# An expert's tail prepares the next expert's split operands, and each expert's code gets a short opening

## The reference, cut to what matters

```
logits = t @ w_router + b_router                 # t: 256 x 1024
top_val, top_idx = top_k(logits, 2); gates = softmax(top_val)
for each expert e, for the tokens x routed to it:
    y = (silu(x @ w_gate_e[e]) * (x @ w_up_e[e])) @ w_down_e[e]     # D_FF = 3584
out[token] += gate * y
```

## Time and profile before

| | before |
|---|---|
| median of three runs | 1839.72 us (1830.52 to 1842.34) |
| the profiled execution | 1832.89 us, of it a span of 1831.1 us |
| mean granted TensorE clock | 0.917 |
| busy: PE, DVE, ACT, POOL | 87%, 39%, 30%, 3% of the span |
| HBM read | 482.66 MB, mean 266 GB/s over the span |
| the chain that ended last | PE 78%, DMA 9%, issue 4%, DVE 4%, ACT 2% |
| idle PE ahead of the eight experts | 5.76, 10.71, 7.29, 0, 7.24, 5.16, 12.38, 5.90 us |

### The profile page before, as it was taken

One profiled execution on the slowest core, in us unless ns is written; L12 is line 12 of the kernel. 1 busy time (PEld: TensorE's weight loads), 2 busy tenths in 40 slices (PEclk: granted clock), 3 DMA queues, 4 the chain that ended last, 5 costly groups with the idle time before them and its releaser, 6 DMA issues.

```text
span 1831.1 us, 30902 instructions
## 1 busy us (share of the span) xinstructions
PE 1598.6 (87%) x12644; PEld 1288.1 (70%) x12645; DVE 710.6 (39%) x1017; ACT 545.7 (30%) x749; POOL 63.2 (3%) x66
## 2 busy tenths in 40 slices
PE   5999997999999999967566799989998749999894
PEld 4777776999987687746344687548897538888552
DVE  2162115555532431140000787116665015666212
ACT  2122114343321321020000676115654015545201
POOL 0010000000000100010000000000000000000002
PEclk8998598999999986898787899999999879999998
DMA  9632255744534133268999999999667997555794
GB/s 364 258 111 97 92 190 206 306 187 170 198 103 188 58 128 137 93 253 362 424 424 425 425 411 389 407 424 377 267 249 278 387 422 327 230 207 230 284 424 167
DMA packets 74563, 488.94 MB, mean 267 GB/s; under 512 B 9792, under 2 KB 13920, under 8 KB 16544
## 3 DMA queue, kind: packets, MB, share of 16 engines
q1 hardware_dynamic: 72176, 479.94, 65.2%
q10 hardware_dynamic: 1648, 4.59, 0.7%
q0 software_dynamic: 576, 2.10, 0.4%
HBM read 482.66 MB, written 3.93 MB: 266 GB/s over the span
## 4 chain that ended last, share of the span: by engine, by line
PE 78%; DMA 9%; issue 4%; DVE 4%; ACT 2%; POOL 1%; SPq 1%; ACTq 0%; POOLq 0%; DVEq 0%
PE PG L1278 9%; DMA arena<-in_experts 5%; PE Y L905 5%; PE PG L1388 4%; PE PG L1322 4%; PE TRB L1322 4%; PE Y L1290 4%; PE Y L1350 4%; PE Y L913 3%; PE Y L1162 3%; PE PG L869 3%; PE PG L870 3%; PE PG L871 3%; DMA ring<-in_experts 3%; PE TRB L1328 3%
## 5 line engine op out<-in xcount | busy, mean ns | idle before, releaser
L1278 PE MATMUL PG<-ring,mixT 128*32 128x128 f32 (+1 forms) x1920 | 115.2, 345 | 63.3 <-issue 63.3
L1471 ACT ACTIVATE parts<-ring 128x2048 fp32r<-128x2048 f32 x84 | 158.5, 1906 | 12.4 <-PE Y L871 8.2
L1278 PEld LDWEIGHTS PG<-ring,mixT 128*32 128x32 f32 (+1 forms) x1920 | 88.6, 136 | 93.6 <-issue 77.9
L2257 DVE COPY arena<-TRB 128x64 f32<-128x64 f32 (+1 forms) x70 | 17.6, 251 | 338.7 <-PE TRB L1264 338.7
L1471 ACT ACTIVATE rope<-PG 64x128 f32<-64x128 f32 (+2 forms) x84 | 27.1, 324 | 376.1 <-PE PG L1278 351.7
L1278 PE MATMUL PG<-arena,mixT 128*32 128x128 f32 (+1 forms) x1664 | 100.3, 349 | 41.7 <-issue 41.7
L869 PE MATMUL PG<-h_parts,parts 128*128 128x256 f32 x448 | 127.5, 285 | 10.2 <-DVE parts L2133 10.2
L870 PE MATMUL PG<-h_parts,parts 128*128 128x256 f32 x448 | 127.3, 284 | 0.0
L871 PE MATMUL PG<-h_parts,parts 128*128 128x256 f32 x448 | 127.1, 284 | 0.0
L1278 PEld LDWEIGHTS PG<-arena,mixT 128*32 128x32 f32 (+1 forms) x1664 | 78.1, 138 | 68.6 <-issue 55.5
L2133 DVE TENSOR_TENSOR parts<-ring,parts 128x2048 fp32r<-128x2048 f32 x42 | 95.9, 2292 | 25.6 <-ACT parts L1471 25.6
(11 more groups left out here) (375 smaller groups left out, 2909.4 us busy)
## 6 DMA issues: line engine op xcount, KB each, us to landing
ring<-in_experts SPq DMA_DIRECT2D x168, 1024.0 KB, 13.0
arena<-in_experts SPq DMA_DIRECT2D x168, 1024.0 KB, 16.4
ring<-in_weights SPq DMA_DIRECT2D x116, 1024.0 KB, 5.8
ring<-in_weights SPq DMA_DIRECT2D x4, 512.0 KB, 4.1
ypairs<-hT ACTq DMA_DIRECT2D x3, 512.0 KB, 5.3
tok<-in_x SPq DMA_DIRECT2D x1, 1024.0 KB, 8.8
result<-scr SPq DMA_DIRECT2D x2, 512.0 KB, 2.6
ring<-in_weights SPq DMA_DIRECT2D x2, 432.0 KB, 6.7
```

The source lines that it names most:

```text
L1278: last = mm(bank[i * n:(i + 1) * n, 0:width], xe[:, k, 0:n], w[k // 4][:, k % 4, i * width:(i + 1) * width], start=(k == 0), stop=(k == KD ...
L1471: return nc.scalar.activation(out_, in_, func, **kw)
```

## The change

Every expert's code becomes two bodies. The six openings lie one behind the other right after the comparisons; behind them lie the six rests. An opening ends in a branch to its own rest, for which a hint is given at the opening's start, and the rest branches to `next` as before.

- PE's opening: whole, the first half (4 of 8 channel blocks) of the first gate-and-up; wide and split, the first unit's high product.
- ACT's opening: whole, the first silu; wide and split, the fourth high part. The first three high parts of an expert are made in the rest of the expert before, ahead of the copy out of `Y`, whatever the next form is (for the first expert, ahead of the loop; behind the eighth, three more, on what the slots hold, which nothing reads). Wide rests begin with a small Silu (`silu_table`).
- DVE's opening: whole, the first product and turned copy, after a wait for the three high parts; wide and split, four low parts. The next expert's tokens (192 columns, `tokens_split`) are parted in the rest of the expert before, ahead of the copy out of `Y`; for 256 the other columns in the opening.
- POOL gathers 64 columns to a buffer of their own (`xe`, for the whole forms), then all 256 to `mixT`; a ninth gather to `mixT` follows.
- PE's whole form waits for the second and third high part in its first two stages, since ACT reads the slots that these stages release.

```diff
         ccol = sb("ccol", [P, KD, 32])
-        s4 = sb("s4", [P, T])
+        strip = sb("strip", [P, 2 * T])
+        s4 = strip[:, 0:T]
...
-        diag = sb("diag", [P, TB, P])
+        diag = strip[:, T:2 * T].rearrange("p (b t) -> p b t", b=TB)
...
-        xe = mixT
+        xe = strip[:, :].rearrange("p (k t) -> p k t", k=KD)
...
-            for n in sorted(NVAR, key=lambda n: n != first_variant):
+            layout = sorted(NVAR, key=lambda n: n != first_variant)
+            for n in layout:
                 with nc.body(label(n), valid_engines=own):
+                    on = eng.mark_branch_hint_location()
+                    emit(eng.snap(turn, min_val=0, max_val=NE - 1), n, True)
+                    eng.br(label(f"rest_{n}")).branch_hint(on)
+            for n in layout:
+                with nc.body(label(f"rest_{n}"), valid_engines=own):
                     back = eng.mark_branch_hint_location()
-                    emit(eng.snap(turn, min_val=0, max_val=NE - 1), n)
+                    emit(eng.snap(turn, min_val=0, max_val=NE - 1), n, False)
                     eng.br(label("next")).branch_hint(back)
             nc.switch_bb(label("done"))
...
+            for i in range(HI):
+                sp.wait_ge(*last_use(i, NE))
+                sp.sem_inc(landed_e[i], 16)
...
-            def expert_whole(e, n):
-
-                def gate_up(s):
-
-                    w = [landed_unit(e, "gu", s, h).rearrange("p (k c) -> p k c", k=KD // 2) for h in range(2)]
+            def expert_whole(e, n, opening):
+                def gate_up(s, halves):
+                    w = {h: landed_unit(e, "gu", s, h).rearrange("p (k c) -> p k c", k=KD // 2) for h in halves}
                     if s >= 2:
                         pe.wait_ge(act_ready, at_unit(e, n, s - 2))
+                    if s < 2 and halves[-1] == 1:
+                        hi_ready(e, s + 1)
+                    if s == 1:
+                        pe.sem_inc(hi_used, USES)
                     bank = PG[:, s % 2, :]
                     width = gate_up_of(n, s)[3]
                     for k in range(KD):
+                        if k // 4 not in halves:
+                            continue
                         for i in range(P // n):
                             last = mm(bank[i * n:(i + 1) * n, 0:width], xe[:, k, 0:n],
-                                      w[k // 4][:, k % 4, i * width:(i + 1) * width], start=(k == 0), stop=(k == KD - 1))
-                    last.then_inc(gu_full, 2)
+                                      w[k // 4][:, k % 4, i * width:(i + 1) * width], start=(k == 0), stop=(k == KD - 1),
+                                      skip_group_check=True)
...
+                        last.then_inc(gu_full, 2)
                 def down(s):
...
+                if opening:
+                    gate_up(0, [0])
+                    return
                 for i in range(STAGES + 2):
                     if i < STAGES:
-                        gate_up(i)
+                        gate_up(i, [0, 1] if i else [1])
                     if 1 <= i <= STAGES:
                         turn(e, n, i - 1, n)
                     if i >= 2:
                         down(i - 2)
-                pe.sem_inc(hi_used, USES)
...
-                pe.wait_ge(x_split, e * 4 + 4)
-                for s in range(STAGES + 1):
+                if opening:
+                    pe.wait_ge(x_split, e * 4 + 6)
+                    gate_up_high(0, 0)
+                    return
+                gate_up_high(0, 1)
+                gate_up_low(0, 0)
+                gate_up_low(0, 1)
+                for s in range(1, STAGES + 1):
                     if s < STAGES:
-                        if s:
-                            pe.wait_ge(act_ready, e * FT + FT + 2 * s - 1)
-                        gate_up_half(s, 0)
-                    if s:
-                        down_rest(s - 1)
+                        pe.wait_ge(act_ready, e * FT + FT + 2 * s - 1)
+                        gate_up_high(s, 0)
+                        gate_up_low(s, 0)
+                    down_rest(s - 1)
                     if s < STAGES:
-                        gate_up_half(s, 1)
-                    if s:
-                        down(s - 1)
+                        gate_up_high(s, 1)
+                        gate_up_low(s, 1)
+                    down(s - 1)
                 pe.sem_inc(tp_full, FT)
...
+                if opening:
+                    pe.wait_ge(x_split, e * 4 + 6)
+                    if n > WIDE:
+                        pe.wait_ge(x_rest, e * 2 + 2)
+                    gate_up_high(0, 0)
+                    return
...
-            def expert(e, n):
-                pe.wait_ge(xe_ready, e + 1)
-                (expert_whole if n < P else expert_split if n % P == 0 else expert_wide)(e, n)
+            def expert(e, n, opening):
+                if opening:
+                    pe.wait_ge(xe_ready, e + 1)
+                (expert_whole if n < P else expert_split if n % P == 0 else expert_wide)(e, n, opening)
...
+            def silu_table():
+                run(rc[0:1, 0, 0:1], rc[0:1, 0, 0:1], ACT.Silu)
...
-            def weights_hi(e, q):
+            def weights_hi(e, q, not_first=True):
                 ae.wait_ge(landed_e[q % SLOTS_E], e * (16 * USES // SLOTS_E) + 16 * (q // SLOTS_E + 1))
-                if q >= HI:
+                if q >= HI or not_first:
                     ae.wait_ge(hi_used, e * USES + (q - HI + 1))
                     ae.wait_ge(conv_lo, e * USES + (q - HI + 1))
...
-            def expert_whole(e, n):
-                for u, s, j, m in units(n):
+            def expert_whole(e, n, opening):
+                for u, s, j, m in units(n)[:1] if opening else units(n)[1:]:
                     silu(e, n, u, m)
-                ae.sem_inc(conv_hi, USES)
+                if opening:
+                    return
+                ae.sem_inc(conv_hi, USES - HI)
                 ae.sem_inc(athi_ready, FT)
                 ae.sem_inc(low_copied, STAGES)
-            def expert_wide(e, n):
...
                     weights_hi(e, expert_at["down", s])
-            def expert_split(e, n):
+            def expert_split(e, n, opening):
                 bl = turns(n)
                 done = HI + 1
-                for q in range(done):
-                    weights_hi(e, q)
...
-            def expert(e, n):
-                (expert_whole if n < P else expert_split if n % P == 0 else expert_wide)(e, n)
+            def expert(e, n, opening):
+                (expert_whole if n < P else expert_split if n % P == 0 else expert_wide)(e, n, opening)
+                if opening:
+                    return
+                for q in range(HI):
+                    weights_hi(e + 1, q)
...
+            for q in range(HI):
+                weights_hi(0, q, not_first=False)
             experts(ae, "act", expert)
...
+            def tokens_split(e):
+                ve.wait_ge(xr_ready, e + 1)
+                c = slice(0, WIDE)
+                V.tensor_copy(h_parts[:, 0, :, c], mixT[:, :, c]).then_inc(x_split, 2)
+                ve.wait_ge(x_split, e * 4 + 4)
+                V.tensor_tensor(h_parts[:, 1, :, c], mixT[:, :, c], h_parts[:, 0, :, c].bitcast(F32),
+                                ALU.subtract).then_inc(x_split, 2)
+            def expert_whole(e, n, opening):
+                if opening:
+                    ve.wait_ge(conv_hi, e * USES + HI)
+                    ve.sem_inc(conv_lo, USES)
+                    ve.sem_inc(x_rest, 2)
...
+                if opening and n > WIDE:
+                    c = slice(WIDE, n)
+                    V.tensor_copy(h_parts[:, 0, :, c], mixT[:, :, c]).then_inc(x_rest, 1)
+                    ve.wait_ge(x_rest, e * 2 + 1)
+                    V.tensor_tensor(h_parts[:, 1, :, c], mixT[:, :, c], h_parts[:, 0, :, c].bitcast(F32),
+                                    ALU.subtract).then_inc(x_rest, 1)
+                elif opening:
+                    ve.sem_inc(x_rest, 2)
                 done = HI + 1
-                for q in range(done):
-                    weights_lo(e, q)
+                if opening:
+                    for q in range(done):
+                        weights_lo(e, q)
+                    return
                 for s in range(STAGES):
                     for i, j, m in bl:
...
-            def expert(e, n):
-                (expert_whole if n < P else expert_split if n % P == 0 else expert_wide)(e, n)
+            def expert(e, n, opening):
+                (expert_whole if n < P else expert_split if n % P == 0 else expert_wide)(e, n, opening)
+                if opening:
+                    return
+                tokens_split(e + 1)
                 ve.wait_ge(down_done, e * FT + 2 * FT)
...
                 last.then_inc(ye_ready, 1)
+            ve.sem_inc(x_split, 2)
+            tokens_split(0)
             experts(ve, "dve", expert)
...
```

(64 more changed lines are left out.)

30 lines of the change are left out of this document (16 added, 14 removed).

## The result

The changed kernel takes 1845.15 us at the median of 20 runs, the kernel before 1839.11 at the median of its 20. The medians lie 6.0 us apart. The ratio of the runs is 1.0043, with an interval of 1.0026 to 1.0059: 8 us slower, where 15 us less were forecast. The profiled executions have spans of 1841.5 and 1831.1 us.

What follows compares the result with a forecast made beforehand. PE, 78% of the chain that ended last, was taken as the bound, with the weights stream bounding some stretches. Terms 1.5 + 0 + 0 + 3.9 + 1.2 + 6.0 + 2.2 = 14.8 us off 1839.72 gave 1825; range 1808 to 1843.

Steps and rivals of the forecast that it cites:

- The step that failed: Whole openings: PE's fetch of the rest runs beside the opening's work, which is the gain: 1.5, 1.2 and 2.2 us.
- the first (1.5): First expert, whole opening: 1.5 us gained of the opening's 1.6, since PE must await the smaller gather; bounds 0 and 5.8.
- the sixth (1.2): Sixth expert, whole opening: a quarter of the two-stage run, 1.2 us, gained; bounds 0 and 5.2.
- the eighth (2.2): Eighth expert, whole opening: a quarter of the two-stage run, 2.2 us, gained; bounds 0 and 5.9.
- Rival C: The second jump behind every opening is paid in full where the hint brings nothing: 7 us slower, 1847; chance 12%.
- The fourth expert: Between third and fourth expert: no gap before, the jump being near; gain 0, or -5 if the rest's code isn't there.
- The term that failed: Fifth expert, ACT: from the end of its copy out to the opening 2.98 us, the near jump's value.
- the 3.9: Fifth expert: PE's second stage starts at 1244.8 instead of 1248.71, 3.9 us gained; bounds 0 and 7.2.
- came of 6.0: Seventh expert: PE's second stage starts at 1516.7 against 1522.72, 6.0 us gained; bounds 2.6 and 12.4.
- the sign I had named for a wrong forecast: Fifth and seventh experts: the forecast is wrong if PE's first stage, and not ACT, sets them; no size given.
- The third expert: PE starts 4 us earlier but waits about 5 us for the silu; own gain 0, bounds -5.2 and +7.3.
- The end: After the eighth expert: ACT's three needless parts (5.7 us) fit in its 6.45 us of idle, costing nothing.

Runs made afterwards that it cites:

- `dve_one_body`: The changed kernel, but DVE has opening and rest of each form in a single body while PE and ACT keep their openings; ratio to the kernel before 0.9994.
- one body: The changed kernel with opening and rest of each form joined into a single body on all engines, the tail's work kept; ratio to the kernel before 0.997.

## Why the prediction was wrong, step by step

**The step that failed** is "its hint is given when the opening starts, about 1.4 us after the load, and the fetch takes what it took. The second half of the first gate-and-up therefore starts where the body starts now." I took the hint to start the fetch, so that it would run beside the opening's work. PE's rest came 7.1 us after the load at the sixth, not 4.9, and DVE's some 5.7 us after its branch, with or without the hint. Of the sum's terms for whole openings, the first (1.5) and the sixth (1.2) turned into -1.7 (with the second) and -3.6; the eighth (2.2) came as 1.8, though by another way: PE stood still for 2.8 us behind the opening, but TensorE's granted clock was 1.00 in its first rows (1725 to 1729 and 1732 to 1737 us), where before it was 0.50 from 1718 to 1721 us, the first part of PE's first run. The sum has no term for the clock.

**What I looked at on one engine only.** The forecast followed PE, and ACT in the split forms. In the whole forms DVE's opening ends in a copy that waits for PE's first turn, so its jump begins only then and the next product stands behind it. That was 4.65 and 4.68 us on PE. `dve_one_body` takes it away, and with it most of the loss by the ratio, but not what was lost at the fourth and fifth. Rival C named a jump "behind every opening", but put its price on ACT and PE.

**The fourth expert.** "No gap now, the jump being near. ... I take 0, with -5 if the rest's code isn't there." It wasn't: 6.3 us from hint to rest, 3.5 us lost.

**The fifth and seventh.** At the fifth ACT's parts stood in the tail as predicted. But ACT's and DVE's ways into the opening, which I took as near from the kernel before, had become far: 5.3 us from its branch to `next` to the load on ACT, and on DVE 2.1 there and 4.7 from the load to the opening. The term that failed is the 2.98 us from ACT's copy out to the opening; ACT was idle for 7.82. PE stood idle for 2.5 us inside its first stage, up to 1246.1 us. Its granted clock was 0.50 from 1246 to 1262 us, and its first stage ended no sooner than ACT was ready: ACT waited 0.26 us for it. Four microseconds of that stage after, then before (20 products for 32), in the columns of the earlier trace rows, and ACT's opening in the fifth and first eviction in the seventh:

```profile
1250.00:1254.00 4.00, 4.00 (x20) 4.00 (x21) 4.00 (x2) 2.08 (x2) 0.00 (x0) 0.50 1.02 418
1240.00:1244.00 4.00, 4.00 (x32) 4.00 (x31) 4.00 (x3) 2.29 (x2) 0.00 (x0) 0.97 1.01 426
1251.90 1.28 ACT L1519 ACT_TABLE_LOAD   x1 [7.82 <-DVE ring_parts L2302]
1532.90 0.49 ACT L1519 ACTIVATE con<-PG 128x384 f32<-128x384 f32 x1 [3.62 <-PE TRB L1354]
```

Counted from PE's branch behind the fourth expert (1226.6 before, 1236.7 after), the second stage began 22.1 us later before and 22.0 after: nothing of the 3.9 was gained. From there to PE's next such branch the expert took 165.5 us for 163.6, as the second stage began at 0.50 of the clock and stayed there up to 1262 us, where before it was 1.00 from 1249 to 1263. Both together make the stretch's 1.5 us lost; that the clock accounts for the second part is an estimate (3.3 us at half speed are worth 1.7). With one body the fifth gains 3.6.

At the seventh PE's opening was far as well (5.2 us from load to hint, and 7.7 more to the rest). Its second stage began 2.8 us earlier than before, counted from PE's branch behind the sixth, and 3.1 us came of 6.0. ACT was ready at 1529.3 and waited 3.62 us for PE's first stage. That is the sign I had named for a wrong forecast: PE's first stage, and not ACT, set the seventh, and at the fifth the two ended together.

**What held.** The third expert gained nothing: PE began earlier and waited for DVE's product behind ACT's silu, 6.74 us, where I had said about 5. The end cost nothing: ACT's needless parts ended 0.82 us ahead of its copy, by the row

```profile
1814.36 0.59 ACT L1519 ACTIVATE hT<-Y 64x512 f32<-64x512 f32 x1 [0.82 <-PE Y L1310]
```

Rival C, 7 us slower at 12%, ended within 2 us of the result. Its mechanism, a second jump paid in full, was the nearest to the right one, and the gap at the fourth expert was its sign; that its sum fits is luck in part, as its other losses fell in other places than it said. The chance I gave it was too low: the far jumps of the kernel before were in the rows, and nothing in them showed a hint at work on a far target.

The Trainium skill, Runtime: NRT & Kernel Launch, section Instruction fetch mechanics, has it that a taken branch to a page outside the current window waits for that page's fetch. The trace agrees with a stall at some targets: from load to body the near ways of the kernel before take 0.6 to 1.4 us and the far ones 3.6 to 7.1, over PE, ACT and DVE.

## What to carry to other kernels

A branch in this kernel is either near or costs some 2 to 7 us on that engine, and rearranging the code changes which ones are near, on each engine differently: look at the sequencer rows (load, compare, hint) of all engines, not at PE's gaps alone. Don't put work that waits for another engine ahead of a far jump: DVE's wait for its code began only when the branch was reached, so the branch belongs ahead of the wait. And look at the granted clock beside each idle stretch that a change moves: at the fifth it was 0.50 for 16 us of work, for some 4 us before. Moving the preparation of the next step into the tail of the last is worth having by itself, and should be measured apart from the change of layout that comes with it.

## What was unexpected

With a hint right ahead of it a far branch was slower on PE by 0.3 to 2.8 us (7.0, 7.5 and 8.0 us with it, 4.8, 7.2 and 5.2 without), and the whole kernel by 0.5% (1.0043 and 0.9989). In the changed kernel the same hint's removal cost 0.7% (1.0117 and 1.0043). Both are shown; why they differ, and how much of either is the code's shift by the hints, stays open.
